# First RMS norm of a four-layer block: halves made from x and the norm's weight, the row factor applied after the projections, first loads reordered

## The reference, cut to what matters

```python
def rms_norm(x, gain):
    y = x * rsqrt(mean(x * x, axis=-1, keepdims=True) + 1e-6)
    return y * gain

def nsa_mixer(h, cos, sin, w_in, ...):           # h = rms_norm(x, norm_mix[0])
    q, kc, vc, ks, vs, kw, vw, gt = split(h @ w_in)
    q, kc, ks, kw = (apply_rope(t, cos, sin) for t in (q, kc, ks, kw))
    ...                                          # kc, vc are compressed in blocks; three attentions
    gates = sigmoid(gt + gate_b)                 # they weigh the three attentions of each head
    ...
```

## Time and profile before

| | |
|---|---|
| median of 3 runs | 2513.81 us (2508.51 to 2514.16) |
| profiled execution | 2505.69 us, its span 2503.9 us, granted TensorE clock 0.997 |
| busy in the span | PE 97%, PEld 81%, POOL 69%, DVE 54%, ACT 34% |

### The profile page before, as it was taken

How to read it: one execution, slowest core, us unless ns; L and a number is a source line. 1 busy time by engine, 2 the same in 40 slices (tenths; PEclk the granted TensorE clock), 3 DMA queues, 4 the chain that set the end, 5 groups by cost and what they waited for, 6 DMA issues and landing times. The chain is left out here.

```text
span 2503.9 us, 34232 instructions
## 1 busy us (share of the span) xinstructions
PE 2433.8 (97%) x11812; PEld 2036.4 (81%) x11812; DVE 1352.7 (54%) x2219; ACT 850.1 (34%) x1828; POOL 1728.6 (69%) x1531
## 2 busy tenths in 40 slices
PE   8989999999999899999999999999999999999998
PEld 7878778888888788888888778888878888888886
DVE  7688846665038656663188865333126445543312
ACT  4667741111028631110056653111015564311102
POOL 7667776666668776666688877666666667766664
PEclk9999999999999999999999999999999999999999
DMA  4300013232322122322322212232322222232322
GB/s 148 127 26 18 26 60 101 92 100 93 101 84 68 43 92 93 99 93 96 101 76 68 76 51 93 92 100 93 101 84 78 68 69 67 85 100 93 100 93 84
DMA packets 58694, 208.61 MB, mean 83 GB/s; under 512 B 6560, under 2 KB 7840, under 8 KB 58592
## 3 DMA queue, kind: packets, MB, share of 16 engines
q1 hardware_dynamic: 58320, 206.88, 25.1%
q10 hardware_dynamic: 272, 0.39, 0.0%
HBM read 205.09 MB, written 2.16 MB: 83 GB/s over the span
## 5 line engine op out<-in xcount | busy, mean ns | idle before, releaser
L725 POOL TENSOR_TENSOR WL<-raw,WH 128x1024 fp32r<-128x1024 f32 x380 | 924.5, 2434 | 64.3 <-ACT WH L2177 15.1
L1057 PE MATMUL PS<-HH,WH 128*128 128x512 f32 x2176 | 855.6, 393 | 13.1 <-POOL HL L948 4.1
L1059 PE MATMUL PS<-HH,WL 128*128 128x512 f32 x2176 | 848.4, 390 | 0.0
L1058 PE MATMUL PS<-HL,WH 128*128 128x512 f32 x2176 | 847.8, 390 | 0.0
L1057 PEld LDWEIGHTS PS<-HH,WH 128*128 128x128 f32 x2176 | 408.6, 188 | 102.6 <-POOL WL L725 6.8
L1059 PEld LDWEIGHTS PS<-HH,WL 128*128 128x128 f32 x2176 | 408.6, 188 | 86.1
L1058 PEld LDWEIGHTS PS<-HL,WH 128*128 128x128 f32 x2176 | 409.0, 188 | 82.1 <-issue 0.5
L713 POOL TENSOR_TENSOR WH<-raw,SC 128x32 fp32r<-128x32 f32 x348 | 95.6, 275 | 458.5 <-DMA raw<-stream 457.8
L714 POOL TENSOR_SCALAR WH<-raw 128x992 fp32r<-128x992 f32 x348 | 361.2, 1038 | 0.0
L1057 PE MATMUL PS<-GH,WH 128*128 (+1 forms) x680 | 264.5, 389 | 0.0
L1058 PE MATMUL PS<-GL,WH 128*128 (+1 forms) x680 | 264.5, 389 | 0.0
(11 more groups left out here) (436 smaller groups left out, 3619.4 us busy)
## 6 DMA issues: line engine op xcount, KB each, us to landing
raw<-stream SPq DMA_DIRECT2D x380, 512.0 KB, 3.5
X<-x SPq DMA_DIRECT2D x4, 512.0 KB, 5.0
out<-X SPq DMA_DIRECT2D x8, 128.0 KB, 1.7
out<-X SPq DMA_DIRECT2D x4, 256.0 KB, 2.0
PR<-params SPq DMA_DIRECT2D x1, 536.0 KB, 8.5
spare_raw_nsa<-stream SPq DMA_DIRECT2D x1, 512.0 KB, 3.4
spare_raw_swa<-stream SPq DMA_DIRECT2D x1, 512.0 KB, 4.5
spare_raw_diff<-stream SPq DMA_DIRECT2D x1, 512.0 KB, 6.0
```

Of the source, the lines that this page charges most:

```text
L725: pool.tensor_tensor(WL[:, w], raw[:, w], WH[:, w].bitcast(F32), ALU.subtract).then_inc(chunk_split, 1)
L1057: pe.matmul(to, h, his[k], start=start and k == 0, stop=False)
L1058: pe.matmul(to, h, los[k], start=False, stop=False)
L1059: last = pe.matmul(to, l, his[k], start=False, stop=stop and k == n_k - 1)
```

## The change

The halves of h are made from x times the norm's weight, without the row factor, so that they need x alone (`first_halves` on ACT, `first_rests` on DVE; the weight is loaded ahead of the parameters into columns of `SC`). The squares, their sum and the root go on beside the first projections: `first_square` on ACT, `first_added` on DVE, `first_sums` on PE in the middle of vc 0, `first_root` on ACT, which leaves the factor in `RF`. DVE multiplies the rotation tables by it (`scaled_tables`) and the tiles without rotation (`scaled_vc`, `scaled_gate`, `scaled_v`), which also copies those tiles out in ACT's place. The tables are loaded again for the second layer after the last rotation of q. `first_chunks` takes the place of `first_two`, the 20 `warm` matmuls go, SP's first loads stand in another order, and four memsets of DVE move from `pad` and the constants to the very start. The semaphore `row_scaled` takes the place of `vc_out`. The diff, cut to its core:

```diff
         HIL = at("HIL", o + 3072, 4 * P, F32R)
+        RF = at("RF", o + 3072, S)
         CS = at("CS", o + 5120, 2 * P)
...
-            for j in range(KT // 2):
+            def load_x(j):
+
                 sp.dma_start(X[:, 2 * j * S:2 * (j + 1) * S], x_in[:, 2 * j * S:2 * (j + 1) * S]
                              ).then_inc(x_landed[j], 16)
+
+            gain = PARAM["norms"] + NORMS[LATE_FIRST][1] * KT
+            sp.dma_start(SC[:, SC_SINK:SC_SINK + KT], params[:, gain:gain + KT]).then_inc(gains_landed, 16)
             for c in range(SLOTS):
                 sp.dma_start(raw[:, c], stream[place_in_stream(c, layers)]).then_inc(raw_landed[c], 16)
-                if c == 1:
+                if c < 2:
+                    load_x(2 * c)
+                    load_x(2 * c + 1)
+                if c == 2:
                     sp.dma_start(PR[:], params).then_inc(inputs_landed, 16)
                     sp.dma_start(IDF[:], consts[:, C_ID:C_ID + P]).then_inc(inputs_landed, 16)
                     sp.dma_start(RC[:], consts[:, C_COS:C_COS + S]).then_inc(tables_landed, 16)
...
                         fetch_spare(n, q["kind"])
+                if q["kind"] == "nsa":
+                    sp.wait_ge(q_roped["nsa"], 8)
+                    sp.dma_start(RC[:], consts[:, C_COS:C_COS + S]).then_inc(tables_landed, 16)
+                    sp.dma_start(RS[:], consts[:, C_SIN:C_SIN + S]).then_inc(tables_landed, 16)
...
                     split(q["proj_chunk"] + 3, c)
+                    pool.wait_ge(tables_landed, 16 * 5)
                     cosines(0)
...
-                    split(0, 2)
-                    norm_lo(0, (1, 3))
-                    split(2, 3)
-                    norm_lo(0, (5, 7))
+                    split(0, 3)
                 else:
...
-            def first_sums(k):
-
-                pe.wait_ge(added, (KT - 2) * (k + 1))
+            def first_sums():
+
+                pe.wait_ge(added, KT - 2)
                 pe.matmul(PS[:, 4], ONE_F[:], WK[:, 4], start=True, stop=False)
+                pe.wait_ge(squared, KT)
+                pe.matmul(PS[:, 4], ONE_F[:], WK[:, 1], start=False, stop=True).then_inc(summed, 1)
+
+            def first_chunks(banks):
+
+                def product(y, t):
+
+                    if t == 0:
+                        pe.wait_ge(chunk_split, y + 1)
+                    if y == 0:
+                        pe.wait_ge(h_lo[t % 2], t // 2 + 1)
+                    last = products(y, PS[:, banks[y]], [h_his[t]], [h_los[t]], 1, t == 0, t == KT - 1, t)
+                    if t == KT - 1:
+                        last.then_inc(chunk_used, 1)
+
+                for t in range(5):
+                    product(0, t)
+                for t in range(5, KT):
+                    product(0, t)
+                    product(1, 2 * (t - 5))
+                    product(1, 2 * (t - 5) + 1)
+                product(1, 6)
+                product(1, 7)
...
-                if k == 0:
-                    first_sums(k)
...
                 else:
-                    first_two(c0, h_wait(k_norm), (proj_bank(0), proj_bank(1)))
+                    first_chunks((proj_bank(0), proj_bank(1)))
                 if nsa:
                     pe.wait_ge(k_out[kind], 1)
-                    proj("vc", 0)
+                    proj("vc", 0, 0, 4)
+                    first_sums()
+                    proj("vc", 0, 4, CT)
                     pe.wait_ge(k_out[kind], 2)
                     proj("vc", 1)
-                    pe.wait_ge(vc_out, 1)
+                    pe.wait_ge(row_scaled, 1)
                     proj("ks", 0)
-                    pe.wait_ge(vc_out, 2)
+                    pe.wait_ge(row_scaled, 2)
                     proj("ks", 1)
...
-                if n == 0:
-                    warm(20)
                 if q["kind"] in MERGED:
...
 
+            def first_halves():
+
+                act.preload_act_table_set(LOG_EXP)
+                act.wait_ge(gains_landed, 16)
+                for t in range(KT):
+                    gain = SC[:, SC_SINK + t:SC_SINK + t + 1]
+                    act.wait_ge(x_landed[t // 2], 16)
+                    act.activation(tile(HH, t), tile(X, t), ACT.Copy, scale=gain).then_inc(h_hi, 1)
+                    if t >= 4:
+                        act.wait_ge(h_lo[t % 2], t // 2 - 1)
+                    act.activation(PS[:, t % 4], tile(X, t), ACT.Copy, scale=gain).then_inc(staged, 1)
+
+            def first_square(t):
+
+                to = WK[:, t // 7] if t in (0, KT - 1) else PS[:, t % 2]
+                if t in (1, 2):
+                    act.wait_ge(h_lo[t % 2], 3)
+                elif 3 <= t < KT - 1:
+                    act.wait_ge(added, t - 2)
+                act.activation(to, tile(X, t), ACT.Square, scale=D ** -0.5).then_inc(squared, 1)
+
+            def first_root():
+
+                act.wait_ge(summed, 1)
+                act.activation(WK[:, 5], PS[:, 4], ACT.Ln, bias=SC[:, SC_EPS:SC_EPS + 1]).then_inc(logged, 1)
+                act.wait_ge(logged, 1)
+                act.activation(RF[:], WK[:, 5], ACT.Exp, scale=-0.5).then_inc(scale_ready, 1)
+
             def norm(k):
...
                         act.wait_ge(mv_turned, before("mv_turned", kind) + i - 1)
-                    if nsa:
-                        act.activation(WK[:, 4 + i % 2], bank, ACT.Copy).then_inc(mv_out, 1)
-                    else:
-                        act.activation(WK[:, 4], bank, ACT.Identity, bias=param("b_qkv", 9)).then_inc(mv_out, 1)
...
                 if nsa:
+                    for t in range(5):
+                        first_square(t)
                     evac_k(0, "kc", 0)
+                    for t in range(5, KT):
+                        first_square(t)
                     evac_k(1, "kc", 1)
-                    for y in range(2):
-                        bank = tile_of("vc", y)
-                        act.activation(O[:, 2 + y], bank, ACT.Copy).then_inc(vc_out, 1)
+                    first_root()
+                    act.wait_ge(inputs_landed, 16 * 2)
                     blocks_first(0)
                     evac_k(2, "ks", 0)
...
                     high(12)
                     high(13)
-                    bank = tile_of("gate")
+                    bank = PS[:, bank_at(kind, "gate")]
+                    act.wait_ge(row_scaled, 3)
                     act.activation(WK[0:48, 5], bank[0:48], ACT.Sigmoid, bias=param("gate_b", 0, 1, 0, 48)
                                    ).then_inc(gate_act, 1)
                     first_k(2)
                     high(14)
-                    evac_v(0, "vs", 0)
                     first_k(3)
                     high(15)
                     evac_cmp(0)
                     high(16)
                     high(17)
-                    act.wait_ge(gate_pe, 1)
-                    evac_v(1, "vs", 1)
                     gelu(0)
                     first_v(0)
                     gelu(1)
                     high(18)
-                    evac_v(2, "vw", 0)
                     first_v(1)
                     high(19)
                     bias_blocks(1)
                     high(20)
                     high(21)
-                    evac_v(3, "vw", 1)
                     first_v(2)
                     evac_q(0)
...
+
+                for t in range(KT):
+                    dve.wait_ge(h_hi, t + 1)
+                    dve.wait_ge(staged, t + 1)
+                    dve.tensor_tensor(tile(HL, t), PS[:, t % 4], tile(HH, t).bitcast(F32), ALU.subtract
+                                      ).then_inc(h_lo[t % 2], 1)
+
+            def first_added():
+
+                for t in range(1, KT - 1):
+                    dve.wait_ge(squared, t + 1)
+                    if t > 1:
+                        dve.wait_ge(added, t - 1)
+                    dve.tensor_tensor(WK[:, 4], PS[:, t % 2], WK[:, 4] if t > 1 else WK[:, 0], ALU.add).then_inc(added, 1)
 
             def halved_down(n, q):
 
...
+
+                def scaled_tables():
+
+                    dve.wait_ge(scale_ready, 1)
+                    own.sig(dve.tensor_tensor(RC[:], RC[:], RF[:], ALU.mult))
+                    own.link(dve.tensor_tensor(RS[:], RS[:], RF[:], ALU.mult))
+
+                def scaled_vc(y):
+
+                    dve.wait_ge(chunk_used, c0 + chunk_at(kind, "vc", y) + 1)
+                    dve.tensor_tensor(O[:, 2 + y], PS[:, bank_at(kind, "vc", y)], RF[:], ALU.mult).then_inc(row_scaled, 1)
+
+                def scaled_gate():
+
+                    dve.wait_ge(chunk_used, c0 + chunk_at(kind, "gate") + 1)
+                    bank = PS[0:48, bank_at(kind, "gate")]
+                    dve.tensor_tensor(bank, bank, RF[0:48], ALU.mult).then_inc(row_scaled, 1)
+
+                def scaled_v(i, part, y):
+
+                    dve.wait_ge(chunk_used, c0 + chunk_at(kind, part, y) + 1)
+                    if i >= 2:
+                        dve.wait_ge(mv_turned, before("mv_turned", kind) + i - 1)
```

(69 more changed lines are left out.)

7 lines of the change are left out of this document (2 added, 5 removed).

## The result

The changed kernel takes 2513.28 us (median of 19 runs, 2511.44 to 2517.94), the kernel before, run beside it, 2510.7 (19 runs). The ratio is 1.0013, 95% interval [1.0007, 1.0019]: 3.3 us slower (1.8 to 4.8), within the 0.3% that was called no change. The forecast was 1.1 us slower, within -1.1 and +3.3. The profiled execution took 2512.28 us, span 2510.4.

The account below looks back on a forecast made before the run. PE was taken to set the pace from 32 us on. Its 8.2 us lead would go to a wait for DVE at the gates, leaving vs 1 1.1 us late: 2513.8 + 1.1 = 2514.9 us, likeliest 2515, range 2505 to 2521.

Parts of the forecast that it names:

- Loads, halves and first products: Kernel start: chunk 0 loaded ahead of x, PE starts at 9.2 us and ends chunks 0 and 1 at 22.0, 9.9 earlier.
- The lead of 8.2 us: End of vc 0: at 29.2 us PE is 8.2 us ahead of before, the most the change can give, 0.33%.
- DVE: Chain from row factor (28.0 us) to gate scaling: `blocks_rest(0)` at 43.0, 32.6 us to `rope_k(5)`'s end, `scaled_gate` 76.3 (74.1 to 78.5).
- The new wait: At the gates' turn: ACT's sigmoid waits for DVE's `scaled_gate`, so PE waits 6.5 us and keeps 1.8 of 8.2.
- From the gates to vs 1: Behind the sigmoid stand `first_k(2)`, `high(14)`, POOL's rest: vs 1 at 83.2 us, 1.1 late, bounds -1.1 and +3.3.
- The clock: Behind PE's wait at the gates: half clock for 3 us loses 1.4 us of work, with 2.9 us to spare.
- The table load: Rival at ACT's sigmoid: the 1.28 us table load runs behind the wait, +2.4, 2516.2 us; chance 0.15.
- The gain: Rival: POOL holds DVE much less, the gate is ready in time, -8.2, 2505.6 us (half 2510); chance 0.11.
- At the start: Rival: the clock falls in PE's thin stretch, 9.9 to 14.4 us; +2.5 to +8.7, 2516 to 2522.5; chance 0.09.

Follow-up runs that it names:

- e6: Changed kernel with SP's first loads in the old order, x first and the chunks behind it; ratio 1.0030 to the kernel before.
- e10: e8 with DVE's split of W2 behind `rest_v(1)` in place of behind `rest_k(3)`; 2498.37 us, ratio 0.9951 to the kernel before.
- e5: Changed kernel with PE's two sums of the squares ahead of vc 0, not in its middle; ratio 0.9984 to the kernel before.
- e2: Changed kernel with ACT's `high(14)` ahead of the gate's sigmoid; ratio 1.0007 to the kernel before.
- e1: Changed kernel with ACT's sigmoid waiting for PE's gate chunk alone and `scaled_gate` left out; ratio 0.9997 to the kernel before.
- e7: e2 plus 33 useless matmuls of PE on an unused bank ahead of the gates' wait; ratio 1.0009 to the kernel before.
- e3: Changed kernel with DVE's `scaled_gate` ahead of `rope_k(4)`; ratio 0.9999 to the kernel before.
- e4: Changed kernel with both `scaled_gate` ahead of `rope_k(4)` and `high(14)` ahead of the sigmoid; ratio 0.9982 to the kernel before.
- e9: e10 with the sums of squares ahead of vc 0 as well; ratio 0.9975 to the kernel before.
- e8: e4 plus `high(10)` ahead of `first_k(0)`, `high(15)` and `evac_cmp(0)` ahead of `first_k(3)`, W2's split behind `rest_k(3)`; ratio 0.9984 to the kernel before.

## Why the prediction was right, and where it was not

- *Loads, halves and first products* held. First product 8.99 (forecast 9.2), last step of chunks 0 and 1 done at 22.4 (22.0), factor ready 28.41 (28.0). e6 shows that 4.7 us of this are the order of loads.
- *The lead of 8.2 us* is real: in e10, with no wait at the gates, PE turns them at 71.39 against 78.79 before, 7.4 us ahead, with 0.5 spent at the gate chunk.
- *DVE* is the term that was mis-sized. `scaled_gate` ends at 80.06 and not at 76.3, past the late bound of 78.5. `blocks_rest(0)` began at 43.87 (43.0, within its bounds). The step that failed is "from there to the end of `rope_k(5)` nothing changes in DVE's program: 81.67 - 49.05 = 32.6 us": the program is the same, its time is not. It took 35.5 us, because three of POOL's subtractions came back to back over the splits of W2 and a rest; e5, where they missed the splits, took 32.4. By the rows the splits alone are 4.2 us longer than before, `blocks_rest` 0.4; `rest_k(1)`, which POOL held before (2.42), is 1.7 shorter, and `rest_k(0)` is held once in both. I had seen the holding in the earlier trace rows and priced it only up to `blocks_rest(0)`.
- *The new wait* was right in place, kind and length: 6.17 us (6.5), put down to ACT's sigmoid, DVE's scaling ahead of it. That the length fits is in part luck: PE came 4 us late as well. It waited 2.09 us at the gate chunk, whose `high(10)` stands behind `first_k(0)`, and the eight matmuls behind that wait stepped 0.43 us in place of 0.23, 1.6 us more. That slow stretch need not belong to the kernel: in e2, whose programs are the same up to there, PE ran at full speed behind a wait of 1.83 us, came 1.9 us sooner, waited 8.04 us at the gates and turned them at the same 80.83. I had looked at that queue only behind the sigmoid.
- *From the gates to vs 1* the sum held: 6.11 us from the turn to vs 1 (forecast 6.2), through `first_k(2)`, `high(14)` and POOL's rest, so the 3.8 us by which DVE was late are the error at vs 1 (86.94 for 83.2). Vs 1 is 4.85 us late, past the bound of +3.3; in time, the ratio gives +3.3 for a forecast of +1.1. That the measured 2513.28 us lie even below the likeliest 2515 is luck: the 2513.8 that I added to was the median of three runs, and 19 runs of before have 2510.7.
- *The clock* fell as said and cost nothing by itself in this kernel, but it took 2.4 of the 2.8 us that PE had to spare before vs 1's weights, and not 1.4 of 2.9: it was low for 6.8 us, 5 of them at work, and not for 3. e2 shows it as the next limit, where it costs 1.9 us.
- *Rivals.* The table load runs ahead of the wait (65.84 and 80.10), so that rival is out. What the Trainium skill says there (page "ScalarE: Activation LUTs", section "Step-by-step: what each stage is for", a load right before its instruction) holds for the order in the program and tells nothing of the wait. The gain did not stay in this order of DVE, but does in e10's. What I had said for it, that POOL has two chunks fewer to split between 43 and 70 us, is not so: six subtractions start there in both kernels, and in the changed one the last three lie back to back. At the start PE's steps were 0.43 us up to 14.2 us, the lower speed, but beside ACT's pace of 1.22 us a tile (three steps are 1.28) this cost 0.4 us at most.

## What to carry to other kernels

When a factor is moved out of the front of a chain, look at who reads it last and what is queued behind that reader on each engine: here a sigmoid behind a long chain of VectorE held up both TensorE and the copies for the next weights, and one edit for each was needed. A stretch of VectorE keeps its length only if GpSimd's work lies over it as before; price it again when either is moved, and place casts and operations with two SBUF operands where GpSimd is idle. A start that is made earlier is worth its microseconds only when every later meeting of the engines has as much slack.

## What the runs showed of the hardware that I had not expected

- At the start TensorE's steps were 0.43 us for 512 columns from 9.95 to 14.2 us, as long as those at 63 us, where the granted clock of the window is 0.50. The column of the clock has 1.00 there, but the trace's first record of the clock, of the full level, is at 14.3 us. The 36 matmuls of 128 columns ahead (1.24 to 9.18 us, 0.22 a step) had not brought the full speed.
- The length of a wait does not tell whether the clock falls. At the gate chunk waits of 2.09 (changed kernel), 2.02 (e1) and 2.27 us (e7) were followed by 3.4 us at half the clock, and waits of 1.83 (e2), 2.01 (e3) and 2.11 us (e4) at the same place by none. In e7 a wait of 1.78 us behind 33 matmuls of 384 columns was followed by another 3.4 us, which began 1.3 us after the wait's end; in e9 and e8 the clock fell within waits of 2.56 and 3.54 us and stayed low for 3.4 and 6.8.
- A cast of VectorE with one operand, 128x256, takes 0.29 us while GpSimd makes no subtraction and 2.37 beside one: it is held like the operations with two. So is the `TENSOR_SCALAR` of the gates, 0.24 us in e10 and 1.92 in e9.
